# Inputs, the x spill and the output laid out in DRAM as one run per partition, in a two-layer hybrid decoder on eight cores

## What is computed

```python
def reference(x, ...):                       # x: (8, 2048, 1024) float32
    for i in range(DEPTH):                   # 2 layers
        h = rms_norm(x, norm1_w[i])
        proj = h @ w_in[i]                   # (b, L, 2564)
        pa, pb, pc, pd = jnp.split(proj, IN_SPLITS, axis=-1)
        ya = gmlp_mixer(pa, ...)             # A: chunks of 128, spatial gating
        yb = ssd_mixer(pb, ...)              # B: conv, Mamba-2 scan, gated norm; has the 4 time step columns
        yc = pool_mixer(pc, ...)             # C: trailing means over 2, 4, 8, 16
        yd = diff_attn_mixer(pd, ...)        # D: causal differential attention, q, k, v
        x = x + concat(ya, yb, yc, yd) @ w_out[i]
        h = rms_norm(x, norm2_w[i])
        x = x + (jax.nn.silu(h @ ffn_w_gate[i]) * (h @ ffn_w_up[i])) @ ffn_w_down[i]
    return x
```

## Time and profile before

| | us |
|---|---|
| median of the runs | 1785.19 |
| profiled execution | 1783.88 |
| its span on the slowest core (core 2) | 1782.3 |
| spans of the 8 cores | 1770.8 to 1782.3 |
| TensorE busy in it | 1655.2 (93%) |
| VectorE, ScalarE, GpSimd busy | 1072.5, 805.4, 629.4 |
| POOL's transfers: packets, MB, share of the 16 DMA engines | 100912, 99.07, 38.9% |
| SP's transfers | 22448, 42.60, 7.4% |

### The profile page before, as it was taken

The page is one execution under the profiler, slowest core; times in us unless marked ns, Lnnn a source line. Parts: engine busy times, 40 slices in busy tenths (PEclk is TensorE's granted clock), DMA queues, the critical chain, the costliest instruction groups (busy, mean ns, idle before and its releaser), DMA issues.

```text
span 1782.3 us, 25117 instructions; the slowest of 8 cores (1770.8 to 1782.3 us)
## 1 busy us (share of the span) xinstructions
PE 1655.2 (93%) x9950; PEld 770.5 (43%) x10140; DVE 1072.5 (60%) x1975; ACT 805.4 (45%) x1222; POOL 629.4 (35%) x835
## 2 busy tenths in 40 slices
PE   3986879999999999999999998999999997999998
PEld 1443434544444444444444443544444443444443
DVE  3787767877633356687775457687753442655555
ACT  1576722446577633334544635144657573211110
POOL 2587843544223322145434432245422321100000
PEclk9996889999999999999999998999999997999999
DMA  7522397115453068913166059901462303584433
GB/s 145 85 48 95 75 169 112 25 16 87 63 104 48 5 115 184 136 23 50 24 95 118 13 107 187 129 4 23 73 107 60 48 1 83 107 154 71 71 47 107
DMA packets 123478, 143.30 MB, mean 80 GB/s; under 512 B 9168, under 2 KB 91616, under 8 KB 123360
## 3 DMA queue, kind: packets, MB, share of 16 engines
q0 software_dynamic: 100912, 99.07, 38.9%
q1 hardware_dynamic: 22448, 42.60, 7.4%
HBM read 223.95 MB, written 16.78 MB: 135 GB/s over the span
## 4 chain that ended last, share of the span: by engine, by line
PE 82%; DVE 7%; DMA 3%; POOL 3%; ACT 3%; issue 1%; SPq 0%; DVEq 0%; POOLq 0%; ACTq 0%
PE ps L528 82%; DVE s_hT L566 2%; DMA s_mix<-w_in 1%; DVE s_x L556 1%; DMA s_x<-xspill 1%; DVE s_x L566 1%; DVE s_ring L556 1%; PE ps L532 1%; ACT s_x L547 1%; ACT s_tmp L547 1%; POOL s_mix L556 1%; DVE s_ring L566 1%; ACT s_pt L547 1%; POOL s_x L556 0%; POOL s_wx L556 0%
## 5 line engine op out<-in xcount | busy, mean ns | idle before, releaser
L528 PE MATMUL ps<-s_hT,s_ring 128*128 128x512 bf16 x2730 | 657.6, 382 | 9.6 <-DVE s_hT L566 3.3
L556 DVE TENSOR_TENSOR s_x<-s_x,ps 128x512 f32<-128x512 f32 (+2 forms) x496 | 317.5, 670 | 181.9 <-PE ps L528 153.9
L528 PEld LDWEIGHTS ps<-s_hT,s_ring 128*128 128x128 bf16 x2816 | 262.1, 98 | 298.9 <-issue 18.3
L528 PE MATMUL ps<-s_act,s_ring 128*128 128x512 bf16 x1361 | 335.1, 382 | 6.4 <-DVE s_act L566 1.9
L547 ACT ACTIVATE s_sg<-ps 128x512 f32<-128x512 f32 x176 | 104.9, 597 | 414.7 <-PE ps L528 414.0
L566 DVE SCALAR_TENSOR_TENSOR s_sg<-s_sg,ps 128x512 f32<-128x512 f32 x176 | 120.0, 685 | 237.7 <-ACT s_sg L547 126.6
L528 PEld LDWEIGHTS ps<-s_act,s_ring 128*128 128x128 bf16 x1408 | 129.6, 98 | 154.5 <-issue 6.2
L528 PE MATMUL ps<-s_hT,s_x 128*128 128x512 bf16 x747 | 178.6, 386 | 12.5 <-DMA s_x<-w_in 9.5
L556 POOL TENSOR_TENSOR s_x<-s_x 128x512 bf16<-128x512 f32 (+2 forms) x116 | 108.2, 933 | 194.1 <-DVE s_x L566 62.6
L566 DVE SCALAR_TENSOR_TENSOR s_act<-s_sg,ps 128x512 bf16<-128x512 f32 x176 | 119.9, 684 | 56.7 <-PE ps L528 54.1
L528 PE MATMUL ps<-s_x,s_k 32*128 32x512 bf16 (+3 forms) x668 | 113.0, 340 | 9.6 <-ACT s_pt L547 2.2
(11 more groups left out here) (217 smaller groups left out, 2115.0 us busy)
## 6 DMA issues: line engine op xcount, KB each, us to landing
s_ring<-ffn_w_gate POOLq DMA_DIRECT2D x20, 1024.0 KB, 15.3
s_ring<-ffn_w_up POOLq DMA_DIRECT2D x20, 1024.0 KB, 14.2
s_ring<-ffn_w_down POOLq DMA_DIRECT2D x20, 1024.0 KB, 10.8
s_x<-w_in POOLq DMA_DIRECT2D x12, 1024.0 KB, 17.1
s_x<-xT SPq DMA_DIRECT2D x8, 1024.0 KB, 8.3
xspill<-s_x SPq DMA_DIRECT2D x8, 1024.0 KB, 14.1
s_x<-xspill SPq DMA_DIRECT2D x8, 1024.0 KB, 10.7
out<-s_x SPq DMA_DIRECT2D x32, 256.0 KB, 4.0
```

Source lines behind the costliest of these rows:

```text
L528: self.op('pe', lambda e: e.matmul(real(out), lhsT, rhs, start=start, stop=stop), [lhsT, rhs], [out], d if dur is None else dur)
L556: self.op(eng, lambda e: e.tensor_tensor(out, real(in0), real(in1), op), [in0, in1], [out], d)
```

## The change

The host lays each tensor out so that what one transfer brings to a partition lies in one run. x, the output and `xspill` become [128, slab, block, 512]; w_out [128, half, 8, 512]; gate, up and w_in are cut into the pieces that are loaded, each of them 8 rows of a partition behind each other. In w_in the pieces stand in the order D, V, B1, B2, A, C, and the four time step columns stand behind v's 256, so that `load_v` is one transfer. Slab 0's first load has 4 parts instead of 8, other first loads 2 instead of 4, and each part has a semaphore of its own. `load_d` waits for block 3 of x instead of block 5; with 4 parts that is the second part, with 8 it was the sixth. `load_b` no longer waits for wV. The computation is the same.

```diff
@@ -661,6 +661,10 @@
+
+WIN = {'d': (0, 512), 'v': (512, 260), 'b1': (772, 512), 'b2': (1284, 512), 'a': (1796, 512), 'c': (2308, 256)}
+WIN_COLS = [(1796, 2564), (1536, 1540), (512, 1536), (0, 512), (1540, 1796)]
+FF_GROUPS = [(j, min(4, NJ - j)) for j in range(0, NJ, 4)]
...
-    x_d = din("xT", [D, L])
-    w_in_d = din("w_in", [2, D, DIN])
-    w_out_d = din("w_out", [2, D, D])
-    wg_d = din("ffn_w_gate", [2, D, DFF])
-    wu_d = din("ffn_w_up", [2, D, DFF])
-    wd_d = din("ffn_w_down", [2, DFF, D])
-    wsT_d = din("gm_wsT", [2, 4, 128, 128])
+    x_d = din("xT", [128, NS, 8, 512])
+    w_in_d = din("w_in", [2, 128, 8 * DIN])
+    w_out_d = din("w_out", [2, 128, 2, 8, 512])
+    wg_d = din("ffn_w_gate", [2, 128, 8 * DFF])
+    wu_d = din("ffn_w_up", [2, 128, 8 * DFF])
+    wd_d = din("ffn_w_down", [2, 128, NJ, D])
+    wsT_d = din("gm_wsT", [2, 128, 4, 128])
...
-    out_d = nc.dram_tensor("out", [D, L], F32, kind="ExternalOutput").ap()
-    xs_d = nc.dram_tensor("xspill", [D, L], F32, kind="Internal").ap()
-    rows8 = lambda ap: ap.rearrange("(c p) t -> p c t", p=128)
-    x_rows, out_rows, xs_rows = rows8(x_d), rows8(out_d), rows8(xs_d)
+    out_d = nc.dram_tensor("out", [128, NS, 8, 512], F32, kind="ExternalOutput").ap()
+    xs_d = nc.dram_tensor("xspill", [128, NS, 8, 512], F32, kind="Internal").ap()
...
@@ -759,12 +761,12 @@
     def load_x(S, s, parts, after=()):
         for hc in range(parts):
             cs = slice(hc * 8 // parts, (hc + 1) * 8 // parts)
-            P.dma('sp', xT[:, S, cs, :], x_rows[:, cs, S * 512:(S + 1) * 512], 'xin%d%d' % (s, hc) if parts == 8 else 'xin%d' % s, rds=after,
+            P.dma('sp', xT[:, S, cs, :], x_d[:, S, cs, :], 'xin%d%d' % (s, hc), rds=after,
                   wrs=[xT[:, S, cs, :]], kb=2048 / parts)
 
 
     P.queue = {}
-    load_x(0, 0, 8)
+    load_x(0, 0, 4)
...
-        load_w(wsTm[:], wsT_d[li].rearrange("h s t -> s h t"), 'wsT')
+        load_w(wsTm[:], wsT_d[li], 'wsT')
...
-        xsrc = x_rows if li == 0 else xs_rows
+        xsrc = x_d if li == 0 else xs_d
...
-        def win_piece(c0, n):
-            return win[:, c0:c0 + n].rearrange("(c p) n -> p c n", p=128)
+        def win_piece(name):
+            off, n = WIN[name]
+            return win[:, 8 * off:8 * (off + n)].rearrange("p (c n) -> p c n", c=8)
...
         def load_d():
-            load_w(wD, win_piece(1796, 512), 'wd', [xT[:, 0, 5, :]] if first else [])
+            load_w(wD, win_piece('d'), 'wd', [xT[:, 0, 3, :]] if first else [])
 
         def load_v():
-            load_w(wV[:, :, 0:256], win_piece(2308, 256), 'wv')
-            load_w(wV[:, :, 256:260], win_piece(1536, 4), 'wv')
+            load_w(wV, win_piece('v'), 'wv')
 
         def load_a():
-            load_w(wA, win_piece(0, 512), 'wa')
+            load_w(wA, win_piece('a'), 'wa')
...
-            pw1 = win_piece(1540, 256)
+            pw1 = win_piece('c')
...
-            load_w(wB1, win_piece(512, 512), 'wb1', after)
-            load_w(wB2, win_piece(1024, 512), 'wb2')
+            load_w(wB1, win_piece('b1'), 'wb1', after)
+            load_w(wB2, win_piece('b2'), 'wb2')
...
             load_d()
             P.dma('pool', cB[:], cb_d, 'cb', wrs=[cB[:]], kb=450)
             load_v()
-            load_x(1, 1, 4, [wD])
-            load_b([wV])
+            load_x(1, 1, 2, [wD])
+            load_b()
             layer_params(li, hb, 28 * KB)
             load_a()
             load_c()
@@ -910,7 +912,7 @@
...
-                    load_x(2 * h + s, s, 4)
+                    load_x(2 * h + s, s, 2)
...
-            load_w(wO[k], w_out_d[li][:, 512 * k:512 * (k + 1)].rearrange("(c p) n -> p c n", p=128), 'wo%d' % k)
+            load_w(wO[k], w_out_d[li][:, k], 'wo%d' % k)
...
-                P.dma('sp', xT[:, S, cs, :], xsrc[:, cs, S * 512:(S + 1) * 512], 'xre%d' % s,
+                P.dma('sp', xT[:, S, cs, :], xsrc[:, S, cs, :], 'xre%d' % s,
...
-            load_w(wg, wg_d[li][:, j0 * 128:(j0 + n) * 128].rearrange("(c p) n -> p c n", p=128), kg)
+            load_w(wg, wg_d[li][:, j0 * KB:(j0 + n) * KB].rearrange("p (c n) -> p c n", c=8), kg)
             wu, ku = piece([8, n * 128])
-            load_w(wu, wu_d[li][:, j0 * 128:(j0 + n) * 128].rearrange("(c p) n -> p c n", p=128), ku)
+            load_w(wu, wu_d[li][:, j0 * KB:(j0 + n) * KB].rearrange("p (c n) -> p c n", c=8), ku)
             wd, kd = piece([n, D])
-            load_w(wd, wd_d[li][j0 * 128:(j0 + n) * 128, :].rearrange("(j p) n -> p j n", p=128), kd)
+            load_w(wd, wd_d[li][:, j0:j0 + n, :], kd)
...
-                        P.dma('sp', xs_rows[:, cs, S * 512:(S + 1) * 512], xT[:, S, cs, :], 'spill%d' % (2 * S + c // 4), rds=[xT[:, S, cs, :]],
+                        P.dma('sp', xs_d[:, S, cs, :], xT[:, S, cs, :], 'spill%d' % (2 * S + c // 4), rds=[xT[:, S, cs, :]],
...
+    def blocks(w, widths):
+
+        out, c0 = [], 0
+        for n in widths:
+            out.append(w[:, :, c0:c0 + n].reshape(2, 8, 128, n).transpose(0, 2, 1, 3).reshape(2, 128, 8 * n))
+            c0 += n
+        return np.ascontiguousarray(np.concatenate(out, axis=2))
+
+    w_in = np.concatenate([f('w_in')[:, :, a:b] for a, b in WIN_COLS], axis=2)
+    ff = [128 * n for j0, n in FF_GROUPS]
...
+        "w_in": blocks(w_in, [n for off, n in WIN.values()]),
+        "w_out": blocks(f('w_out'), [512, 512]).reshape(2, 128, 2, 8, 512),
+        "ffn_w_gate": blocks(f('ffn_w_gate'), ff),
+        "ffn_w_up": blocks(f('ffn_w_up'), ff),
+        "ffn_w_down": np.ascontiguousarray(f('ffn_w_down').reshape(2, NJ, 128, D).transpose(0, 2, 1, 3)),
+        "gm_wsT": np.ascontiguousarray(f('gm_ws').transpose(0, 3, 1, 2)),
...
-        m["xT"] = np.ascontiguousarray(x[b].T)
+        m["xT"] = np.ascontiguousarray(x[b].reshape(NS, 512, 8, 128).transpose(3, 0, 2, 1))
```

More of the change, by code:

```diff
@@ L1309, in mixing @@
             w_out(s)
-    groups = [(j, min(4, NJ - j)) for j in range(0, NJ, 4)]
+    groups = FF_GROUPS
     cnt = {'ring': 0, 'act': 0, 'sg': 0}
@@ L1399, in host_pack @@
     cf, cb = make_consts()
-    return {
-        "w_in": np.ascontiguousarray(f('w_in')),
-        "w_out": np.ascontiguousarray(f('w_out')),
-        "ffn_w_gate": np.ascontiguousarray(f('ffn_w_gate')),
-        "ffn_w_up": np.ascontiguousarray(f('ffn_w_up')),
-        "ffn_w_down": np.ascontiguousarray(f('ffn_w_down')),
-        "gm_wsT": np.ascontiguousarray(f('gm_ws').transpose(0, 1, 3, 2)),
+    def blocks(w, widths):
[6 more added lines that the diff above has]
+    ff = [128 * n for j0, n in FF_GROUPS]
+    return {
+        "w_in": blocks(w_in, [n for off, n in WIN.values()]),
[4 more added lines that the diff above has]
+        "gm_wsT": np.ascontiguousarray(f('gm_ws').transpose(0, 3, 1, 2)),
         "gm_bs": np.ascontiguousarray(f('gm_bs')),
@@ L1427 @@
         m = dict(shared)
-        m["xT"] = np.ascontiguousarray(x[b].T)
+        m["xT"] = np.ascontiguousarray(x[b].reshape(NS, 512, 8, 128).transpose(3, 0, 2, 1))
         in_maps.append(m)
     res = run_bass_kernel_spmd(nc, in_maps, core_ids=list(range(8)))
-    out = np.stack([np.asarray(res.results[b]["out"], dtype=np.float32).T for b in range(8)], axis=0)
+    out = np.stack([np.asarray(res.results[b]["out"], dtype=np.float32).transpose(1, 3, 2, 0).reshape(L, D) for b in range(8)], axis=0)
     return out
```

2 lines of the change are left out of this document (1 added, 1 removed).

## The result

| | before | after |
|---|---|---|
| median of the runs, us | 1785.19 | 1808.06 |
| profiled execution, us | 1783.88 | 1809.44 |
| spans of its 8 cores | 1770.8 to 1782.3 | 1771.0 to 1807.9 |
| POOL's transfers: packets, share of the 16 DMA engines | 100912, 38.9% | 16624, 32.9% |
| VectorE, ScalarE, GpSimd busy | 1072.5, 805.4, 629.4 | 1061.8, 809.2, 593.7 |

The kernel became slower by a factor of 1.0125 (95% interval 1.0096 to 1.0155). The factor compares fast runs alone, 1785.0 and 1785.19 before with 1806.34, 1806.68 and 1809.44 after, and leaves out slow ones at 1816.41 and 1924.97 before and at 2015.61 after. The forecast of 1770 (1752 to 1790) was wrong. The page of after, to be held against the earlier trace rows: span, TensorE, its granted clock in tenths, and the two queues.

The account below looks back on a forecast made before the run. TensorE was taken as the bound, busy 1655.2 of 1782.3 us. Start-up 11.6 plus reloads 3.8, other terms 0, took 15.4 off 1783.9 to 1768.5; with the median 1.3 higher the forecast was 1770 us, range 1752 to 1790.

Parts of the forecast that it names:

- Longer runs: Weight transfers, one run per partition instead of 8 or 4: no gain in steady state, 0 us.
- nearly the same busy share: Sign of being right: profile's third section shows about an eighth of the packets on q0, busy share nearly unchanged.
- Start-up: First weight loads: V's matmuls start at 29.0 instead of 40.65, winning 11.6 us, ends 4 and 16.6.
- x transfers: Loads of x in fewer, larger parts with own semaphores: the last part still decides, 0 us.
- Reloads: x from xspill after layer 1's attention lands earlier beside weight transfers: 3.8 us won, ends 0 and 11.4.
- The sum without the order: Whole kernel: start-up 11.6 plus reloads 3.8, 15.4 us off the profiled execution.
- New order: Planner's changed instruction order on every engine: no sign known, so 0, with 8 us either way.
- given back: Rival, chance 0.19: start's win lost again as slab 1's norm or x is late; 1778 to 1782 us.
- Clock: Rival, chance 0.10: earlier weights and new order close half the idle and low-clock loss at 140-210 us; 1752 us.
- Blocked reload: Rival, chance 0.07: layer 1's x reload waits until both weight transfers finish; 1774 us, or 1784 with a third.
- Slow cast: Rival, chance 0.07: casting weight transfers with 4096-element descriptors run at half today's rate; 1795 us, at factor 3 1880.

Follow-up runs that it names:

- e1: The kernel after with before's transfers and instruction order, so only the DRAM layout differs from before; median 1868.17 us, lowest execution 1781.49.
- e3: The kernel after with all its layout and transfers, but before's instruction order on every engine; 1780.16 us, ratio 0.9922 to before.
- e2: The kernel before, matrices kept plain, with after's transfers and instruction order and V as one transfer; 1787.66 us, ratio 1.002 to before.
- e7: e3 with x of slabs 2 and 3 first loaded in four parts, as in before; ratio 0.9906 to before.
- e4: The kernel after with one edit undone, load_b waiting for wV again; ratio 0.9901 to before.
- third group: Follow-up kernels run together on one chip, after among them; after took 1785.17 us there, ratio 1.0003 to before.
- e10: e4 with the planner's transfer cost changed to 2.5 us and 240 KB per us, so only the order differs; 1741.63 us, ratio 0.9753 to before.
- e14: e4 with the planner's transfer cost changed to 2.25 us and 235 KB per us, so only the order differs; ratio 0.9773 to before.
- second group: Follow-up kernels run together on one chip, e4 and e7 among them; the kernel before took 1802.93 us there.

## Why the prediction was wrong, step by step

- **Longer runs, 0 in steady state.** The step's reading of the DMA queues was off: I expected "nearly the same busy share", and POOL's share fell from 38.9% to 32.0% on a quiet core (about 693 to 567 us of engine time for the same 99.07 MB). The packets fell to a sixth (16624 of 100912), not an eighth. For the kernel, e1 holds this term and the reloads together, 0 and -3.8 in the forecast: it has -1.5 in the table of work, -6.5 in its one quiet mean and -7.8 by its fastest cores, so a few us are missing here, and where they come from is open.
- **Start-up, -11.6.** Right in kind and some 3 us too large. e3 shows -10.9 at 10 us of work and -8.3 lasting. The 40.65 of the working is from core 2, the latest: V started at 33.9 to 40.6 on before's cores and at 24.3 to 29.9 on after's, 9 us sooner on average. On cores 2, 7 and 3 of after V started at 26.2 to 27.4 (forecast 29.0) and D at 18.5 to 21.2 (forecast 23). It is the transfers that did it, not the layout: e2 has -10.3 and e1 -0.9.
- **x transfers, 0.** In the old order right to 3 us (-8.7 to -11.7 in the table between 550 and 900, not traced further). In the new one wrong: I had looked only at the reloads of layer 1, and it was that of layer 0 that grew, from 4.7 us of VectorE's wait to 11.3 (core 7).
- **Reloads, -3.8.** Sign and size were right: behind 900 us of work, which ends ahead of the reloads of layer 1, e3 goes from -11.7 to -15.1. VectorE's waits for xspill on core 3, of before and of e3 (sum, number, longest):

```profile
DVE s_x L556 <- DMA s_x<-xspill: 16.2, 2, 10.0
```

```profile
DVE s_x L566 <- DMA s_x<-xspill: 12.9, 2, 7.9
```

The working had a slip that hides in the result. It counts two weight transfers of 1.05 MB ahead of the last reload, but the one issued at 1492.91 has half of that (DMA issues of before, 1491 to 1494):

```profile
s_ring<-ffn_w_down POOLq DMA_DIRECT2D x1, 512.0 KB, 7.8
```

With 1.57 MB the same sum ends at 1505.7, 5.0 us earlier than before instead of 2.5. The good size is in part luck.

- **The sum without the order, -15.4**, is what e3 (-15.1 in the table, -17.4 in quiet means), e7 (-17.0) and e4 (-17.6) measured. The undisturbed executions of e3 are at 1765 to 1770.
- **New order, 0 with 8 either way.** This is the step that failed. It was +16 to +18 on quiet cores; the rest of the 38 us between forecast and result is the stretches at 0.81. "I have no sign for that" was the fault, and so was the measure: idle time bounds what a new order can win, not what it can lose. Where before had none, from 460 to 620 us, the new order made 5.8 us of it on core 7 and took the clock down. A sign was to be had, since the planner's own end rose from 1731.9 to 1746.1. Orders of this program span 22 to 60 us.
- **The rival "given back"** (0.19, 1778 to 1782) was the mechanism of the first loss, 12 us between 42 and 70: slab 1's norm is late, the squares at 48 instead of 37.6, and slab 0's attention is not work in hand for TensorE but a chain through ScalarE and POOL. It was priced as a loss of the start alone; the larger one around 510 to 670 it did not have. Quiet executions of after are at 1782 to 1788. So the range up to 1790 would have held in the third group (1785.17) with the same wrong step in it.
- **Clock** was given 17 us in the other direction, and no case had a loss by it. The 0.81 stretches put 20 to 30 us on top on the first chip; no row of before's profiled execution showed them. What brings them is open.
- **Blocked reload**: whole transfers do not block, packets alternate. **Slow cast**: fell; transfers with long runs land sooner (ffn_w_gate 13.7 us against 15.3).

## What to carry to other kernels

When an edit feeds a scheduler, split it before anything else: the old list with the new transfers (e3) took one kernel and separated -17 from +17. If the scheduler has a model of its own, read how it ends for both lists; it was 14 us worse here, and one removed wait made all of it. Other constants of the model were worth 26 us (e4 to e10, in different groups), more than the layout and the transfers (17); but the lowest end of 124 settings (e14) was not the fastest kernel. A faster or earlier transfer is not free for the one beside it: ask which load on the critical path shares the engines with it.

## What was not expected of the hardware

- Two queues with 8 KB packets share the DMA engines one packet to one (96 to 97), and the casting one takes 63% of the time for the same bytes written, the plain one 34%.
- Weights in 1024 short runs sent their first packet 4.7 us after their issue (644.25 to 648.95) while SP's queue ran; those in 128 long runs after 2.4 us. This head start is what delayed x.
- One run per partition takes 18% less engine time than runs of 2 and 4 KB (567 against 693 us), though the rate of 2 KB packets in the earlier trace rows was no better than that of 1 KB ones in the earlier trace rows.
- A pair of cores together may be granted 0.81 of the clock for 160 us, starting 3 to 7 us after TensorE goes from 1.2 GHz to dense work; in the second group the stretches were only 3 to 15 us long and more in number. A long one costs about 30 us.
